# A convolution tap moved to ScalarE and a modulation piece moved out of the first projection

## The reference, cut to what matters

```python
def causal_depthwise_conv(x, w, b):          # 4 taps, 1536 channels
    k_w, ch = w.shape
    y = lax.conv_general_dilated(x, w[:, None, :].astype(x.dtype), window_strides=(1,),
                                 padding=[(k_w - 1, 0)], dimension_numbers=('NWC', 'WIO', 'NWC'),
                                 feature_group_count=ch)
    return y + b

def mixer_ssd_mla(h, ...):
    z, xbc, dt_raw, q_a, kv_a, k_pe = split_cols(h @ w_in, L0_SIZES)
    xbc = jax.nn.silu(causal_depthwise_conv(xbc, conv_w, conv_b))
    ...

def swiglu(h, w_gate, w_up, w_down):
    return (jax.nn.silu(h @ w_gate) * (h @ w_up)) @ w_down

def adaln_modulation(c, w, b):
    mod = jax.nn.silu(c) @ w + b
    return [m[:, None, :] for m in jnp.split(mod, N_MOD, axis=-1)]
```

## Time and profile before

| | |
|---|---|
| median of 3 runs | 2032.34 us (2029.23 to 2037.05) |
| the profiled execution | 2031.83 us, its span 2030.0 us |
| TensorE busy | 1905.8 us, 94% |
| VectorE busy | 1393.6 us, 69% |
| ScalarE busy | 986.7 us, 49% |
| GpSimd busy | 256.3 us, 13% |
| mean granted TensorE clock | 0.978 of full speed |

### The profile page before, as it was taken

The page is one execution under the profiler, slowest core; times in us unless marked ns, Lnnn a source line. Parts: engine busy times, 40 slices in busy tenths (PEclk is TensorE's granted clock), DMA queues, the critical chain, the costliest instruction groups (busy, mean ns, idle before and its releaser), DMA issues.

```text
span 2030.0 us, 33216 instructions
## 1 busy us (share of the span) xinstructions
PE 1905.8 (94%) x13188; PEld 1757.2 (87%) x13188; DVE 1393.6 (69%) x2530; ACT 986.7 (49%) x1432; POOL 256.3 (13%) x118
## 2 busy tenths in 40 slices
PE   6899799988998889998998899999999999999998
PEld 6887699978977679998997889999998888999997
DVE  6898765557956574336756548988878887666665
ACT  6445544454435364446554445566653334444444
POOL 0001044420001024440000057000000000000000
PEclk9999999999998899999999999999999999999999
DMA  8654476646564245555443444477776866555453
GB/s 323 229 184 150 147 253 244 241 168 217 198 212 161 73 159 186 187 185 192 158 151 133 141 146 151 170 224 215 211 218 238 305 244 226 195 221 197 177 199 113
DMA packets 94232, 392.79 MB, mean 193 GB/s; under 512 B 7648, under 2 KB 41584, under 8 KB 55552
## 3 DMA queue, kind: packets, MB, share of 16 engines
q1 hardware_dynamic: 94080, 390.69, 55.3%
HBM read 372.83 MB, written 15.73 MB: 191 GB/s over the span
## 4 chain that ended last, share of the span: by engine, by line
PE 76%; DVE 13%; ACT 3%; issue 2%; DMA 1%; POOL 0%; DVEq 0%; SPq 0%; ACTq 0%
PE ps L563 10%; PE ps L564 10%; PE ps L565 10%; PE acc L559 9%; PE acc L560 9%; PE acc L561 9%; PE acc L563 3%; PE acc L565 3%; PE acc L564 3%; DVE wlo L1292 2%; PE ps L1247 1%; PE acc L1247 1%; DVE arena L1321 1%; PE ps L1018 1%; PE ps L629 1%
## 5 line engine op out<-in xcount | busy, mean ns | idle before, releaser
L2336 ACT ACTIVATE whi<-raw 128x1024 fp32r<-128x1024 f32 x559 | 590.7, 1059 | 496.7 <-PE acc L561 273.5
L1292 DVE TENSOR_TENSOR wlo<-raw,whi 128x1024 fp32r<-128x1024 f32 x463 | 572.2, 1242 | 301.3 <-ACT whi L2336 298.5
L563 PE MATMUL ps<-hhi,whi 128*128 128x256 f32 x1824 | 523.9, 287 | 10.2 <-ACT hhi L2450 6.8
L564 PE MATMUL ps<-hlo,whi 128*128 128x256 f32 x1824 | 519.4, 285 | 0.0
L565 PE MATMUL ps<-hhi,wlo 128*128 128x256 f32 x1824 | 519.1, 285 | 0.0
L563 PEld LDWEIGHTS ps<-hhi,whi 128*128 128x128 f32 x1824 | 352.9, 193 | 15.9 <-ACT hhi L2450 7.9
L564 PEld LDWEIGHTS ps<-hlo,whi 128*128 128x128 f32 x1824 | 353.3, 194 | 2.9
L565 PEld LDWEIGHTS ps<-hhi,wlo 128*128 128x128 f32 x1824 | 353.0, 194 | 0.0
L1292 POOL TENSOR_TENSOR wlo<-raw,whi 128x1024 fp32r<-128x1024 f32 x96 | 239.0, 2492 | 638.2 <-ACT whi L2336 637.9
L559 PE MATMUL acc<-whi,chi 128*128 128x512 f32 x752 | 295.9, 393 | 3.5 <-DVE wlo L1292 1.9
L560 PE MATMUL acc<-whi,clo 128*128 128x512 f32 x752 | 294.6, 392 | 0.0
(11 more groups left out here) (445 smaller groups left out, 2385.6 us busy)
## 6 DMA issues: line engine op xcount, KB each, us to landing
raw<-in_peer_down SPq DMA_DIRECT2D x64, 1024.0 KB, 5.0
raw<-in_peer_up SPq DMA_DIRECT2D x64, 1024.0 KB, 5.1
arena<-in_ada SPq DMA_DIRECT2D x80, 512.0 KB, 4.9
raw<-in_w_gate SPq DMA_DIRECT2D x22, 1024.0 KB, 4.9
raw<-in_w_up SPq DMA_DIRECT2D x22, 1024.0 KB, 4.8
raw<-in_w_down SPq DMA_DIRECT2D x22, 1024.0 KB, 4.8
arena<-spill SPq DMA_DIRECT2D x14, 1024.0 KB, 7.1
spill<-hT_t SPq DMA_DIRECT2D x22, 448.0 KB, 6.4
```

Source lines behind the costliest of these rows:

```text
L563: e.matmul(out, hi, xh, start=start, stop=False, skip_group_check=True)
L564: e.matmul(out, hi, xl, start=False, stop=False, skip_group_check=True)
L1292: e.tensor_tensor(out=lo, in0=w, in1=hi.bitcast(F32), op=ALU.subtract).then_inc(*X(("lo", j)))
L2336: e.activation(hi, w, ACT.Copy, scale=1.0).then_inc(*self.A(("hi", j)))
```

## The change

The first tap with the bias goes from VectorE to ScalarE: an ACTIVATE Identity with `conv_w` as scale and `conv_b` as bias, for each of the 12 channel tiles, directly behind the eviction of the strip. It waits for that eviction; VectorE's tap 2 waits for it. ScalarE's `rstd` instructions in strip 0 and its silu stand behind it.

`w_low` 0 loses its `eager` call on both engines, and `w_up0` 5 gains one. Nothing else of the modulation is edited.

```diff
     def pe_proj0(self, e):
         for i in range(3):
-            self.pe_linear(e, "w_low", i, 8, 2, m.hH, m.hL, None if i else "mix0", eager=True)
+            self.pe_linear(e, "w_low", i, 8, 2, m.hH, m.hL, None if i else "mix0", eager=i > 0)
...
     def pe_ffn(self, e, layer):
...
-            self.pe_linear(e, f"w_up{layer}", i, 8, 2, m.hH, m.hL)
+            self.pe_linear(e, f"w_up{layer}", i, 8, 2, m.hH, m.hL, eager=(layer, i) == (0, 5))
...
     def ve_proj0(self, e):
         for i in range(3):
-            self.ve_linear(e, "w_low", i, 8, 2, eager=True)
+            self.ve_linear(e, "w_low", i, 8, 2, eager=i > 0)
...
-            for k in (3, 2, 1, 0):
+            for k in (2, 1, 0):
                 for j in (2 * i, 2 * i + 1):
-                    if k == 3:
-                        e.tensor_scalar(out=m.xc[:, j, :], in0=m.xb[:, j, 3:259], scalar1=m.pv("conv_w", 4 * j + 3, 1),
-                                        scalar2=m.pv("conv_b", j, 1), op0=ALU.mult, op1=ALU.add).then_inc(
-                                            *V(("conv", j, k)))
...
+                    e.wait_ge(*self.at("conv", j, k + 1))
+                    e.scalar_tensor_tensor(out=m.xc[:, j, :], in0=m.xb[:, j, k:k + 256],
...
     def ve_ffn(self, e, layer):
...
-            self.ve_linear(e, f"w_up{layer}", i, 8, 2)
+            self.ve_linear(e, f"w_up{layer}", i, 8, 2, eager=(layer, i) == (0, 5))
...
     def se_proj0(self, e):
         for i in range(6):
             self.se_linear(e, "w_xbc", i, 8, 2, m.xb[:, 2 * i:2 * i + 2, 3:259])
+            e.wait_ge(*self.at("out", "w_xbc", i))
+            for j in (2 * i, 2 * i + 1):
+                e.activation(m.xc[:, j, :], m.xb[:, j, 3:259], ACT.Identity, bias=m.pv("conv_b", j, 1),
+                             scale=m.pv("conv_w", 4 * j + 3, 1)).then_inc(*A(("conv", j, 3)))
```

7 lines of the change are left out of this document (2 added, 5 removed).

## The result

| | before | after |
|---|---|---|
| median of 12 runs, us | 2031.04 | 2039.0 |
| lowest to highest | 2027.26 to 2037.41 | 2034.53 to 2044.44 |
| profiled execution (its span) | 2031.83 (2030.0) | 2044.44 (2042.7) |
| mean granted clock of it | 0.978 | 0.974 |

The changed kernel is slower: 1.0037 times the time before, with a 95% interval from 1.0026 to 1.0049, some 7.5 us. The forecast was 2032.0, no change. The time is at the upper end of the forecast's range (2026 to 2039). The profiled execution of the changed kernel is the slowest of its twelve, 5.4 us above their median, while that of before is 0.8 us above its own. Some of what its trace shows is therefore not the rule, and the traces of the experiments are needed to tell which.

What follows compares the result with a forecast made beforehand. The chain of waits was three quarters TensorE, with VectorE setting the pace in the convolution. Gains of 11.5 and losses of 11.2 us summed to -0.3 us on the profiled 2031.83; forecast median 2032.0, range 2026 to 2039.

Steps and rivals of the forecast that it cites:

- first projection: In w_low, one piece fewer ahead of the cut, L694 moved to mid-strip of w_low 2: 2.7 us off, bounds 1.5 and 3.1.
- convolution: In the w_xbc strips, twelve first taps leave VectorE and are hidden on ScalarE: 3.5 us off, bounds 3.9 and 0.
- `w_z` strips: Two L694 groups move from strip starts to mid-strip and wait for pieces: 5.4 us lost, bounds 2.4 and 7.
- call 20: In MLA's w_out0a, L694 moves between second and third strip of rows and waits for a piece: 2.8 us lost.
- gate rows: In MLA, two pieces are made ahead of them, L694 finds its sum late: 2.8 us lost, bounds 1.2 and 5.
- `mix1`: Second layer's first stage: L694 no longer waits 4.49 us, but the strip behind still needs a cut; 0.3 us off.
- inside GLA and its end: Inside GLA perhaps 0.2 us lost; at its end the 4.71 us wait shrinks, 4.0 us off.
- `ffn1`: In FFN 1, an L694 falls into TensorE's gap of 2.17 us ahead of the first strip: 1.0 us off.
- sum: All terms over the whole kernel: -0.3 us on the profiled execution's 2031.83 us; chance 0.60 to land within 4 us.
- the rival of the late taps: In the convolution, ScalarE's taps become the bound, steps stay at 7.0 us, 3.5 us of gain go: 2035.5; chance 0.10.
- my slack of 0.3: In the convolution, ScalarE's first taps would be ready 0.3 us before VectorE comes to them.
- the clock falls in the new holes: TensorE's clock falls in four new waits, 2.4 us each, one us less won at GLA's end: 2042.6; chance 0.13.

Runs made afterwards that it cites:

- zback: Kernel before, w_low 0's piece left out and made up for by one more call at the end of the SSD; 2043.08 us against 2031.29, ratio 1.0054.
- zbacktap: Kernel before, w_low 0's piece left out and made up for at the SSD's end, first tap on ScalarE; 2040.76 us against 2032.25, ratio 1.0031.
- warm: Changed kernel with 16 matmuls of ones ahead of the waits of calls 12, 16, 20 and 24; 2040.24 us against before's 2030.91, ratio 1.0043.
- pieces: Kernel before with both call edits (w_low 0 out, w_up0 5 added), first tap left on VectorE; 2043.33 us against 2030.91, ratio 1.0048.
- warm10: Changed kernel with 10 matmuls of ones ahead of the waits of calls 12, 16, 20 and 24; 2040.08 us against before's 2031.29, ratio 1.0036.
- first: Kernel before with only the piece of w_low 0 left out; 2050.97 us against 2032.52, ratio 1.0081.
- mend: Changed kernel with one more call in w_xbc 0 on both engines; 2029.56 us against before's 2032.52, ratio 0.9980.
- low2: Changed kernel with the piece left out of w_low 2 and not of w_low 0; 2039.97 us against before's 2032.25, ratio 1.0038.
- zskip: Kernel before with the piece left out of the last w_z strip only; 2034.50 us against 2030.91, ratio 1.0016.
- ffn: Kernel before with only the added call in w_up0 5, on both engines; 2028.27 us against 2032.52, ratio 0.9973.
- tapffn: Kernel before with the first tap on ScalarE and the added call in w_up0 5, nothing left out; 2027.23 us against 2030.91, ratio 0.9973.
- tap: Kernel before with only the first tap moved to ScalarE; 2030.14 us against 2032.52, ratio 0.9989.

## Where the prediction was right and where wrong

The mechanism was right: both engines' counters shift all later calls, and the loss comes from where L694 then stands. The waits appeared at every place named, at 2.65 and 2.50 us for "3 and 1", 2.69 for 2.4 and 3.26 for 3. Wrong were sizes, and with a sum that was a difference of two numbers near 11, seven misses of the same sign out of eight made "no change" into slower. By terms, first that of the prediction, then what the kernels with the same edit have in common:

| term | forecast | measured | in |
|---|---|---|---|
| first projection | -2.7 | about 0 | after -0.3, zback -0.6, zbacktap -0.8, warm +0.6, pieces +0.9, warm10 +1.3, first +1.6, mend +3.0, start included |
| convolution | -3.5 | -2.2 to -2.5 | eight kernels; -0.7 in after |
| `w_z` strips | +5.4 | +6.5 (9.3 without the tap) | after, low2, zbacktap; first, pieces, zback |
| call 20 | +2.8 | +4.4 | after, pieces, zskip; 5.7 in first, low2 |
| gate rows | +2.8 | +3.3 | after, pieces, zskip; 4.9 in first, low2 |
| `mix1` | -0.3 | -1.2 | after, low2, pieces, ffn; -0.2 to -0.9 without the added call |
| inside GLA and its end | -3.8 | -3.0 | ffn, mend, low2, pieces, warm; +0.4 in after |
| `ffn1` | -1.0 | -1.6, and +1.8 back behind it | after, ffn, mend, tapffn, pieces, low2, warm |
| sum | -0.3 | +7.9 | the ratio gives +7.5 |

**The first projection is the step that failed by most.** "In mid-strip L694 then waits for the fourth piece, which ends at about that time, around 55": it ended at 57.93. I moved the pieces and left their loads where they were. My own rows had VectorE's piece waiting for its load at 605.23 and at 226.44, and I took that into account there and not here. `low2` shows the 4.5 us. The other half of the step was right: in `first`, `mend` and `pieces` `w_low` 2 starts 12.6 to 12.7 us behind `w_low` 0 instead of 15.1, so 2.5 us of the 2.7 that I had taken off are there, and then L694 waits 1.9 to 2.1 us in mid-strip for the late piece. In the profiled execution of the changed kernel `w_low` 0 itself ran partly at a fallen clock (7.3 us instead of 5.8), VectorE waited for a high part behind it, and `w_low` 2 started only 0.7 us earlier than before, at 54.11:

```profile
48.31 1.23 DVE L1292 TENSOR_TENSOR wlo<-raw,whi 128x1024 fp32r<-128x1024 f32 x1 [2.14 <-ACT whi L2331]
```

**The convolution**: the step of 6.4 us, the order on ScalarE and the 3.5 us on VectorE were right (3.66). TensorE takes 2.5 up to the end of its last strip. The step that failed is that the whole gain outlasts the next stage: I moved VectorE's instructions of `w_z` against GpSimd's two products there and priced nothing for it, and in `tap` that took 1.06 us back. In the profiled execution of the changed kernel the rival of the late taps came true in one step. TensorE's wait ahead of `w_xbc` 2, ScalarE's eviction and VectorE's first own tap:

```profile
79.82 0.35 PE L563 MATMUL acc<-hhi,whi 128*128 128x256 f32 x1 [2.28 <-DVE wlo L1292]
...
87.34 0.60 ACT L2343 ACTIVATE arena<-acc 128x512 f32<-128x512 f32 x1 [1.60 <-PE acc L565]
...
88.68 2.49 DVE L1624 SCALAR_TENSOR_TENSOR arena<-arena,pv_t 128x256 f32<-128x256 f32 x6 [1.49 <-ACT arena L2533]
```

The strip took 7.48 us at a fallen clock, the eviction came late, and the taps behind it: 1.49 us of wait against my slack of 0.3. The four other kernels with ScalarE's taps and the piece left out of the first projection (`low2`, `zbacktap`, `warm`, `warm10`) don't show it.

**The `w_z` strips**: from VectorE's start of the stage, L694 was forecast at 1.5 and came at 1.6, the decays' end at 7.6 and came at 7.55, the second strip's at 16.6 and came at 16.2. The clamp took 3.01 us where the row of before had 2.17; that is most of the last 1 us. The clamp runs beside GpSimd's second product there, and four multiply-adds beside the first:

```profile
120.89 1.91 POOL L2931 TENSOR_TENSOR arena<-arena 128x1024 f32<-128x1024 f32 x1 [120.45 <-ACT arena L2549]
120.29 4.71 DVE L1321 SCALAR_TENSOR_TENSOR arena<-arena,gs_t 128x512 f32<-128x512 f32 x4
129.40 2.35 POOL L2931 TENSOR_TENSOR arena<-arena 128x1024 f32<-128x1024 f32 x1 [6.60 <-ACT arena L2549]
```

The 1.5 us of the multiply-adds are mostly hidden, as the forecast had VectorE wait for TensorE there.

**Call 20**: the wait was right (2.69 for 2.4), the clock was not in it. It fell in all five kernels with an unfilled hole there, L694 at 2.07 to 2.08 us. In `first` and `low2` nine matmuls behind it stayed at 0.43 us each instead of two, which makes their 5.7. That is the rival "the clock falls in the new holes", which I had at 0.13 with four fallen clocks and 2042.6 us. It came true at one of the four holes, and with VectorE's taps at two. Its condition, "at half after holes of 2.4 to 3 us", is too simple: 3.26 us at the gate rows never fell in any kernel.

**Gate rows**: 2.6 for 2.8 up to the rows themselves; 0.9 more stand behind them, where `w_out0b` waits 1.82 us for a cut.

**mix1 and FFN 1**: both signs right, both gains larger, though part of the one in `mix1` is in kernels without the added call too. The gain of FFN 1 was given back behind it. In `ffn` 1.4 us of that stand behind a wait of 2.41 us, where two strips lasted from 1111.14 to 1123.97, 12.8 us, and 11.4 in the kernel before (1114.38 to 1125.79). `after`, `pieces` and `warm` have these 12.8 too, and so has `first`, without the added call; `mend`, `tapffn` and `low2` have 11.4 and lose as much some 50 us later. Why all seven end with 1.7 to 2.1 us lost stays open.

**The profiled execution's extra 5 us** are two such draws: 1.5 in the convolution, and 3.4 in GLA and its end, where `after` and `tapffn` have +3.6 and -3.2 and five others +1.9 and -4.8. The draw in GLA is the clock's: behind the same wait of 3.62 us for a cut (579.31 in `after`) the granted clock of the next 20 us was 0.74 in these two and 0.83 in `ffn`, `mend`, `low2` and `pieces`, and at the end of GLA L694 took 1.99 and 1.87 us in these two and 1.16 in those four.

**The range** reached to 2039 because of the clock's rival, and the median is 2039.0. The first projection's term lay outside its bounds (1.5 to 3.1 us off, and it was 0), since none of them had the load in it; the convolution's lay within (0 to 3.9), near which I had taken the favourable end.

## What to carry to other kernels

When a program numbers its background work by calls, dropping one call moves all that follow. Find for every later group whether it falls at the start of a strip or in its middle, and whether its last piece's load is the one held by the ring: here the same edits cost 7.5 us or gained 4, by one call more or less, and one call too many cost 24. Move the loads in the sum too, not only the arithmetic. A gain on the engine that sets the pace moves all its later instructions against those of the other engines: here 1.06 of 3.66 us went where two of them came to stand beside GpSimd's. And when gains and losses of 11 us each are set off against each other, the answer is no surer than the worst of them.
